# Low expert rows added on VectorE, the last stage's loads held behind the first fetch, and a piece of the p projection moved ahead of the picked tokens

## What is computed

```python
h = h + mixed @ w_o[i]
f = rmsnorm(h, ffn_norm_g[i])
...
top_vals, top_idx = lax.top_k(f @ router_w, 2)      # two of eight experts per token
h = h + sum over the two experts of gate * ((silu(f @ w1[e]) * (f @ w3[e])) @ w2[e])
gate = jax.nn.sigmoid(rmsnorm(h, ple_norm_g[i]) @ ple_gate_w[i])
h = h + gate * (p[i] @ ple_proj_w[i])
```

## Time and profile before

| | us |
|---|---|
| median of three runs | 1708.97 |
| the profiled execution | 1711.69 |
| its span | 1709.8 |
| TensorE busy | 1695.3 (99%) |
| VectorE busy | 1378.6 (81%) |
| ScalarE busy | 1231.2 (72%) |
| GpSimd busy | 59.2 (3%) |

### The profile page before, as it was taken

One profiled execution on the slowest core, in us unless ns is written; L12 is line 12 of the kernel. 1 busy time (PEld: TensorE's weight loads), 2 busy tenths in 40 slices (PEclk: granted clock), 3 DMA queues, 4 the chain that ended last, 5 costly groups with the idle time before them and its releaser, 6 DMA issues.

```text
span 1709.8 us, 24926 instructions
## 1 busy us (share of the span) xinstructions
PE 1695.3 (99%) x8555; PEld 1415.4 (83%) x8555; DVE 1378.6 (81%) x1607; ACT 1231.2 (72%) x1564; POOL 59.2 (3%) x43
## 2 busy tenths in 40 slices
PE   9999999999999999999999999999999999999998
PEld 7877779898888889888888888888888888888786
DVE  5667876777774577699899898899898998989995
ACT  6667665665553566887888887887877878878775
POOL 0002100000000000000000000000000000000301
PEclk9999999999999999999999999999999999999999
DMA  9942354369645453299999999999999999999993
GB/s 320 345 182 95 110 193 172 123 227 419 247 179 215 154 203 148 105 393 380 373 397 372 376 386 372 379 397 365 385 386 376 388 375 370 402 370 386 380 375 123
DMA packets 76948, 510.60 MB, mean 299 GB/s; under 512 B 8312, under 2 KB 8440, under 8 KB 19537
## 3 DMA queue, kind: packets, MB, share of 16 engines
q1 hardware_dynamic: 67792, 479.45, 72.3%
q0 software_dynamic: 6496, 25.52, 4.6%
q10 hardware_dynamic: 2592, 4.72, 0.7%
HBM read 485.02 MB, written 24.64 MB: 298 GB/s over the span
## 4 chain that ended last, share of the span: by engine, by line
PE 94%; DVE 2%; DMA 1%; ACT 1%; issue 1%; ACTq 0%; SPq 0%; POOL 0%; DVEq 0%; POOLq 0%
PE ps L1990 23%; PE ps L1995 22%; PE ps L1991 22%; PE ps L2397 6%; PE ps L1954 4%; PE ps L2404 3%; PE ps L2376 1%; PE ps L2375 1%; PE ps L2382 1%; PE ps L1983 1%; PE ps L1975 1%; PE ps L1979 1%; DVE wlo L1271 1%; DMA raw<-in_w_fixed_dram 1%; PE ps L2291 1%
## 5 line engine op out<-in xcount | busy, mean ns | idle before, releaser
L1271 DVE TENSOR_TENSOR wlo<-raw,whi 128x1024 fp32r<-128x1024 f32 x886 | 1028.1, 1220 | 130.3 <-ACT whi L760 129.2
L760 ACT ACTIVATE whi<-raw 128x1024 fp32r<-128x1024 f32 x886 | 882.4, 1053 | 119.5 <-PE ps L1995 84.6
L1990 PE MATMUL ps<-whi,xgh 128*128 128x512 f32 x896 | 353.6, 395 | 0.0
L1991 PE MATMUL ps<-whi,xgl 128*128 128x512 f32 x896 | 348.9, 389 | 0.0
L1995 PE MATMUL ps<-wlo,xgh 128*128 128x512 f32 x896 | 276.7, 390 | 1.6 <-DVE wlo L1271 1.5
L1995 PEld LDWEIGHTS ps<-wlo,xgh 128*128 128x128 f32 x896 | 167.9, 188 | 38.2 <-DVE wlo L1271 2.8
L1990 PEld LDWEIGHTS ps<-whi,xgh 128*128 128x128 f32 x896 | 168.3, 188 | 34.2 <-ACT whi L760 0.4
L1991 PEld LDWEIGHTS ps<-whi,xgl 128*128 128x128 f32 x896 | 168.4, 188 | 33.4
L1990 PE MATMUL ps<-whi,mTh 128*128 128x512 f32 x448 | 175.9, 393 | 0.0
L1991 PE MATMUL ps<-whi,mTl 128*128 128x512 f32 x448 | 174.4, 389 | 0.0
L1995 PE MATMUL ps<-wlo,mTh 128*128 128x512 f32 x448 | 138.1, 389 | 0.0
(11 more groups left out here) (418 smaller groups left out, 1952.6 us busy)
## 6 DMA issues: line engine op xcount, KB each, us to landing
raw<-in_w_moe_dram SPq DMA_DIRECT2D x336, 1024.0 KB, 7.2
raw<-in_w_fixed_dram SPq DMA_DIRECT2D x112, 1024.0 KB, 5.1
tokens_scratch<-zeros POOLq DMA_DIRECT2D x1, 8704.0 KB, 44.6
y_scratch<-zeros POOLq DMA_DIRECT2D x2, 2304.0 KB, 57.6
y_scratch<-yo ACTq DMA_DIRECT2D x18, 256.0 KB, 6.0
xin<-tokens_scratch SPq DMA_DIRECT2D x8, 512.0 KB, 7.3
bias_scratch<-revb POOLq DMA_DIRECT2D x1, 3072.0 KB, 38.1
raw<-in_w_fixed_dram SPq DMA_DIRECT2D x4, 512.0 KB, 4.6
```

Of the source, the lines that this page charges most:

```text
L760: AC(whi[:, v % SPL, c], raw[:, v % RAW, c], ACT.Copy).then_inc(high_done, 1)
L1271: V.tensor_tensor(wlo[:, v % SPL, c], raw[:, v % RAW, c], whi[:, v % SPL, c].bitcast(F32), ALU.subtract).then_inc(low_done, 1)
L1990: mm(o, hi(k0 + k, T), wh[:, k, :], start=first and k == 0, stop=False)
L1991: mm(o, lo(k0 + k, T), wh[:, k, :], start=False, stop=False)
```

## The change

Seven edits. (1) GpSimd no longer scales and adds the low rows; VectorE does it with one operation per token tile, placed between its splits in the last expert. (2) SP waits for `y_fetched0` before the four loads of the last stage. (3) Row block 0 of `y_scratch` is zeroed early by two DMAs of GpSimd, beside the other zeros, and ScalarE's two stores ahead of round 0 become two semaphore increments. (4) `late_p(1, 1)` stands ahead of the picked tokens on TensorE, and its copy ahead of the conversion of the picked tokens on ScalarE. (5) In `last_ple` VectorE does `add_last(1)` before the split of unit ple1+2, and `turned_low(6, 1)` before that of ple1+3. (6) Unit ple1+1 is multiplied in the order high, low weights, low activations, and `second_rows` stands in its second half, ahead of the last four matmuls. (7) The four matmuls of L2619 are gone.

```diff
@@ sync
             g.post = True
+            sp.wait_ge(y_fetched[0], 32)
             for j, unit in enumerate(after):
                 load(U["ple1"] + j, unit)
@@ gpsimd
+                        pool.dma_start(y_dram[half][0:1].rearrange("a p n -> p (a n)"), zeros[:, 0:NB])\
+                            .then_inc(rows_cleared, 16)
...
-            pool.wait_ge(rows_cleared, 48)
+            pool.wait_ge(rows_cleared, 80)
...
-            pool.wait_ge(low_fetched, 64)
-            for T in range(NT):
-                ins = pool.tensor_scalar(y_low[:, T, :], y_low[:, T, :], gk[:, 0, T:T + 1], None, ALU.mult)
-            ins.then_inc(low_scaled, 1)
-            pool.wait_ge(low_scaled, 1)
-            pool.tensor_tensor(h[:], h[:], y_low[:], ALU.add).then_inc(low_added, 1)
@@ scalar
-            split_gathered(0)
             act.wait_ge(half_used, 2 * U["p1"] + 2)
             AC(p_late[:, 1, 1], ps[:, 3, :], ACT.Copy).then_inc(p_copied, 1)
+            split_gathered(0)
...
-            act.wait_ge(y_copied, 2)
             for half in range(2):
-                store(half, 0)
+                act.sem_inc(rows_stored[half], 16)
@@ vector, expert (last round)
+                    for T in range(NT):
+                        dve.wait_ge(low_fetched, 64)
+                        V.scalar_tensor_tensor(out=h[:, T, :], in0=y_low[:, T, :], scalar=gk[:, 0, T:T + 1],
+                                               in1=h[:, T, :], op0=ALU.mult, op1=ALU.add).then_inc(low_added, 1)
+                        split_to(ub + 4 * NFB + 6 + T + AHEAD)
                     split_to(ub + UNITS_ROUND - 1)
-                    dve.wait_ge(low_added, 1)
+                    dve.wait_ge(low_added, 2)
                     add_last(0)
@@ vector, last_ple
+                add_last(1)
                 split_to(ub + 2)
-                add_last(1)
+                turned_low(6, 1)
                 split_to(ub + 3)
-                turned_low(6, 1)
@@ tensor, products
+                        if half and before_low:
+                            before_low()
                         pe.wait_ge(low, n_parts)
@@ tensor, last_ple
-                products(ub + 1, KU, NB, *X, 0, outs[1], True, False)
-                second_rows()
-                for _ in range(4):
-                    mm(ps[:, 6, :], order[:, 1, :], whi[:, (ub + 1) % SPL, 0:NB], start=True, stop=True)
+                products(ub + 1, KU, NB, *X, 0, outs[1], True, False, norm=6, before_low=second_rows)
@@ tensor, ahead of the first expert
+            late_p(1, 1).then_inc(half_used, 2)
             pe.wait_ge(pick_done, 1)
             pe.wait_ge(h_normed, 1)
...
-            late_p(1, 1).then_inc(half_used, 2)
```

More of the change, by code:

```diff
@@ L360, in build @@
         low_fetched = sem("low_fetched")
-        low_scaled = sem("low_scaled")
         low_added = sem("low_added")
@@ L777, in root @@
                 if k == 3:
-                    act.wait_ge(rows_cleared, 48)
+                    act.wait_ge(rows_cleared, 80)
                 for i in range(NT):
@@ L1630, in mix @@
                 if i:
-                    dve.wait_ge(rows_cleared, 48)
+                    dve.wait_ge(rows_cleared, 80)
                 if i == 0:
@@ L1959, in split_view, with products @@
                         wlo[:, s, 0:nk * n].rearrange("p (k n) -> p k n", k=nk))
-            def products(u, nk, n, hi, lo, k0, outs, first, last, middle=None, halves=(0, 1), norm=None):
+            def products(u, nk, n, hi, lo, k0, outs, first, last, middle=None, halves=(0, 1), norm=None,
+                         before_low=None):
                 wh, wl = split_view(u, nk, n)
```

## The result

The changed kernel took 1713.90 us (median of 10 runs), the kernel before 1709.77 us beside it (10 runs). The ratio is 1.0021, with a 95% interval of 1.0013 to 1.0029: slower by 0.2%, where 0.2% faster was forecast. The profiled execution has a span of 1712.0 us; before it was 1709.8. The spans differ by 2.2 us and the medians by 4.1, since the profiled execution of the kernel before (1711.69 us) is longer than its median.

The account below looks back on a forecast made before the run. TensorE's dense matmul stream bounds the kernel (94% of the span), so only its standstills and last-stage row waits matter. Savings 1.65 + 0.5 + 0.95 = 3.1 us from 1708.97 gave 1705.9 us, range 1703.9 to 1708.5.

Parts of the forecast that it names:

- Low rows: Last expert: with the low rows on VectorE, its splits speed up and TensorE's wait goes; 1.65 us won (1.5 to 1.8).
- p piece: Start of first expert: p projection's last part ahead of picked tokens, ScalarE's stores gone; 0.5 us won (0 to 0.8).
- the hold: Tail: SP's four last-stage loads wait for the first half's fetches; with VectorE's new order, 0.95 us won (-0.1 to 2.1).
- the size of the descriptor pass: First half's fetch in the tail: two GpSimd passes of 1.5 us each (0.95 to 2.1), landing at 1670.6.
- the 3.2 us of cover: Last expert: VectorE's splits end about 1672.2, TensorE wants the dependent rows at 1675.4; without this cover, up to 2.6 us lost.
- the clock: Rival at the last stage's start: half clock behind the idle gap, 1.5 us lost, 0.9 net, 1706.8 us; chance 0.13.
- the 0.6 us wait for the second fetch: Tail: TensorE ready at 1690.9 for the second turn of rows, which starts at 1691.5.
- The hold buys nothing: Rival, tail: first half's fetch still lands at 1676.2, tail loses 4.65 us instead of winning 0.95; 1711.5 us; chance 0.08.
- Descriptors are not faster with VectorE idle: Rival, second half's fetch: the 3.17 us pass does not shrink, second turn 2.2 us later, 1708.1 us; chance 0.08.
- the loads slow the fetch: Tail: last-stage loads share DMA engines with the first half's fetch; 9.01 us to land, 3.5 with queues free.

Follow-up runs that it names:

- run with early rows: Changed kernel with VectorE's two low-row operations moved to two earlier hidden blocks of the last expert, SP's wait kept; 1710.32 us, ratio 1.0005 to the kernel before.
- run with no hold: Changed kernel without SP's wait for the first half's fetches, all else kept; 1708.79 us, ratio 0.9994 to the kernel before.
- the run of 2.75: Kernel before with only the p part ahead of the picked tokens, ScalarE's stores replaced by counts, and the zero rows; 1710.11 us, ratio 0.9998.

## Why the prediction was wrong

**Low rows and p piece: right.** 1.65 and 0.5 were forecast, 2.15 together; 2.47 came, of which the p piece 0.7 and the rows 1.8 (from the first turned hidden block to ScalarE's copy 913.60 us before, 911.78 after).

**The failed step: the hold, at two of its terms.** The first is the size of the descriptor pass: "VectorE is busy here, so I take 1.5 each (bounds 0.95 and 2.1)". The first pass took 6.82 us. The bounds came from passes beside a VectorE close behind ScalarE, and the same change put it further behind: the price of the row operations was looked for in what TensorE wants of VectorE (the 3.2 us of cover held), not in what GpSimd needs beside VectorE. The fetch was ready at 1672.11 + 2.47 = 1674.6 instead of 1670.6, and the last stage started at 1684.9 instead of 1680.9 on the old clock: 4.0 us. The pass itself is 5.3 us over its term; 0.9 came back because the store landed in 4.31 us instead of 5.25, and 0.5 because the second pass took 0.96.

Five profiles with ten splits in 11.51 us have first passes of 5.9 to 6.8 us; nine with nine splits in 10.81 us, the kernel before among them, have 1.0 to 2.1. In the five, whenever the pass began, it ended 0.85 us after the start of the stream's last split, when VectorE had caught up with ScalarE. It would be natural to say that small waits of VectorE let GpSimd through, but the kernel before speaks against it. Its pass is over at 1664.75 + 2.09 = 1666.84, while VectorE's splits still follow straight on each other; the first wait, 0.13 us, comes ahead of the last split shown here:

```profile
1664.73 1.22 DVE L1271 TENSOR_TENSOR wlo<-raw,whi 128x1024 fp32r<-128x1024 f32 x1
1665.87 1.22 DVE L1271 TENSOR_TENSOR wlo<-raw,whi 128x1024 fp32r<-128x1024 f32 x1
1667.05 1.23 DVE L1271 TENSOR_TENSOR wlo<-raw,whi 128x1024 fp32r<-128x1024 f32 x1
1668.41 1.23 DVE L1271 TENSOR_TENSOR wlo<-raw,whi 128x1024 fp32r<-128x1024 f32 x1
```

What differs is how far VectorE is behind ScalarE: at the first split that starts during the pass, 0.2 to 0.4 us in the nine and 0.9 to 1.0 in the five. How this holds GpSimd up is not shown.

The Trainium skill, "SBUF — State Buffer", section "Who interferes with whom", infers that a VectorE instruction with two SBUF inputs does not hold up the making of descriptors. The trace disagrees: 6.82 us under such a stream, 0.95 with VectorE idle.

The second is the clock, which the sum left out and a rival priced at 1.5 us, 0.9 net. It cost 2.26 us, at most 0.1 of it hidden: VectorE's second addition ended at 1692.54, and TensorE would have been there at 1694.69 - 2.26 = 1692.43. The run with early rows, whose tail is the one forecast, has it as well: with the pass as sized, the forecast would still have failed on this. The Trainium skill, "TensorE: Matmul & The Clock Gate", section "HAM oscillation — how this bites in real kernels", has waits for data bring the half clock; the trace agrees, with a granted clock of 0.50 behind the gap of 6.37 us.

On the two profiled executions the sum closes: forecast -3.1; rows and p -0.3; late fetch +4.0; clock +2.26; and the 0.6 us wait for the second fetch, which was in the sum and did not occur, -0.6. That is +2.2, the difference of the spans. The ratio says 3.6. The forecast took it that the saving is the same on the profiled execution and on the median; that did not hold, and the other 1.4 us are not explained.

**The rivals.** "The hold buys nothing" came nearest. Its turning point, a landing at 1673.7, was passed by 0.9 us, and for the reason it named, a fetch slow without the loads; at 0.08 its chance was too low. "Descriptors are not faster with VectorE idle" is refuted: 0.95 and 0.96 us in the second half, as forecast, and in the kernels that kept the old order there 1.97 and 3.17 us for the first. That the loads slow the fetch was right (7.78 us beside them, 3.56 alone), but the answer overshot: two of the four loads were wanted at once, and only the other two could wait.

## What to carry to other kernels

Hold back only the transfers that are wanted late: against the run with no hold the same wait made the kernel 0.27% slower ahead of the first load and, if anything, 0.14% faster ahead of the third. When work is moved onto an engine, ask also which engine works beside it at that moment: here GpSimd's first descriptor pass went from 2.09 to 6.82 us. And price a new gap of TensorE of several microseconds at its length and the half-clock start behind it.

## What the hardware showed unexpectedly

A descriptor pass that takes 0.95 us with VectorE idle took 5.9 to 6.8 us beside ten back-to-back splits, and ended with them, not a fixed time after its start. The half clock appeared behind gaps of TensorE of 2.75, 3.73, 3.9, 4.14 and 6.37 us, and not behind those of 2.28 and 2.71; in the run of 2.75 it came when the matmuls had already resumed. It also accounts for some of the scatter between executions of one kernel: ahead of the first expert some profiles have it and some do not, with the same program there up to line numbers (the changed kernel, then the run with early rows):

```profile
719.00:720.00 1.00, 1.00 (x4) 0.50 1.06 451
```

```profile
719.00:720.00 1.00, 1.00 (x9) 1.00 1.00 426
```

The picked tokens start 1.5 us apart for it (722.52 and 721.02); at the first turned hidden block 1.1 us of that is left (30.87 and 29.74 us after the router's matmuls).
